# The q, k and v tiles of a hybrid block in pairs by seven block products, the head rows' work among the state-space tiles

## The chip, the cores and the metric

One core of a Trainium2 chip runs the whole block. The metric is the device time of one execution in microseconds (us). Five engines work side by side, each with its own queue, in the order of its program: TensorE (PE, matrix products into PSUM), VectorE (DVE), ScalarE (ACT), GpSimd (POOL) and SyncE (SP, which issues DMAs). They wait for each other by semaphores. SBUF is the working memory of 128 partitions; PSUM has 8 banks of 128 x 512 floats.

## The reference

The block normalises x (1024 tokens x 1024 channels), projects it by one wide matrix `w_in`, and splits the result. The stretch of interest is the projection and the causal convolution behind it, for the state-space branch (`xbc`) and for the DeltaNet branch (`qkv`):

```python
h = rms_norm(x, g_mix_pre[i])
proj = h @ w_in[i]
z, xbc, dt_raw, qkv, gate, b_raw, a_raw, m_gate = jnp.split(proj, IN_SPLITS, axis=-1)
xbc = jax.nn.silu(causal_dwconv(xbc, conv_w) + conv_b)      # 4 taps, 1536 channels
qkv = jax.nn.silu(causal_dwconv(qkv, conv_w))               # 4 taps, 3072 channels
dt = jax.nn.softplus(dt_raw + dt_bias)                      # and g, beta of DeltaNet from a_raw, b_raw
```

Then come the two chunked recurrences, their gated merge, a gated convolutional feed-forward part and a per-layer input embedding. All is float32.

## The kernel before

**Precision and tiles.** Every operand of a product is split into a high and a low part (`w_hi`, `w_lo` of the weights, `act_hi`, `act_lo` of h, all in SBUF), and a product is three matmuls: high x high, high weight x low activation, low weight x high activation. A tile is 128 output channels x 1024 tokens: 8 blocks of 128 input channels x 2 halves of 512 tokens x 3 = 48 matmuls of 512 columns, into one of four buffers of two PSUM banks (`pe_unit`, `pe_steps`, lines 465 to 489).

**Per tile.** SP loads 1 MB of weights for two tiles (`load_block`). POOL makes the high part (line 460) and then the low one (line 462). PE multiplies. DVE copies the tile from PSUM into `xin`, which has three zero columns in front (line 2895), so that the buffer is free at once; the first tap is a `tensor_scalar` on it (line 2902), the other three are `scalar_tensor_tensor` (line 2908) over `xin` and `ring_a`. ACT applies SiLU (line 2813) and stores the tile to the `spill` tensor in DRAM, two in rotation (`spilled`).

**Order.** `PROJ` gives it: 12 state-space tiles, then q and k (16 tiles), v in two runs of 4; all but the first four tiles run in hardware loops of four (`run_tiles`). The head rows (one small tile with dt, a and b in its rows) go through a softplus on DVE (`head_softplus`, 16 dependent operations in `hrow`) behind tile 11; PE turns them to token rows behind q and k (`O_TM`), DVE keeps them (`tm_sources`); PE sums them over the tokens of a chunk behind the first run of v (`O_CUM`), DVE keeps that (`tm_sums`), ACT takes four exponentials. The numbers `O_...` say which use of the four buffers a tile is, `U_...` which use of the weight slots, `Q_...` of the load slots.

**Behind it** (`pe_a`, `dve_a`, `act_a`, `sp_a`, `pool_a`): the z, gate and merge-gate tiles on PE, with the preparation of DeltaNet between their steps. It reads q, k, v of one chunk of tokens back from `spill`, which SP does once all 36 tiles are stored; the first steps of PE that need it stand 15 steps (1.9 tiles) into this stage (`A_START`).

**A stage of the same kind as the change.** The feed-forward stage (`pe_tail`, lines 1820 to 1870) already multiplies its gate and up tiles in pairs by seven products: a matrix of 2 x 2 blocks (output channels x input channels) times one of 2 x 2 blocks (input channels x halves of the tokens) with seven block products instead of eight. Four of the seven weights are sums of weight blocks (`sm`, by DVE, line 2372), ACT makes the high part of each (line 2085), POOL the low one (line 1735). Four of the seven activations are sums of blocks of h, made once (`t1` to `t4`, lines 2349, 2055, 2354). DVE adds the seven products, each one PSUM bank, into the two tiles by seven additions (line 2390), with one product first copied by ACT (`sx`, line 2092). There, ACT takes the first of three taps (line 2068), DVE two (line 2403), on every second pair; on the others DVE multiplies (line 2414).

## Time and profile before

| | |
|---|---|
| median of 3 runs | 2575.64 us (2573.89 to 2580.5) |
| the profiled execution | 2580.09 us, span 2578.4 us |
| PE busy | 2473.8 us, 96% |
| DVE busy | 1541.1 us, 60% |
| POOL busy | 1205.1 us, 47% |
| ACT busy | 720.9 us, 28% |
| DMA | 339.42 MB, mean 132 GB/s |
| PE clock granted | 0.986 of full speed over the span |

The profiled execution is one of its own, and its span leaves out what lies around the program. Busy shares are means over stages with different limits; a wait counts only where it ends last. In the timeline, a matmul's duration overlaps that of the next, so the distance between starts tells its cost. Three stretches matter here: the state-space tiles (69.7 to 200.3 us), q, k, v (200.3 to 461), and the stage behind.

### The profile page before, as it was taken

How to read it: one execution, taken by the hardware profiler on the slowest of the kernel's cores; microseconds unless marked ns; L12 is line 12 of the kernel's file. 1: busy time of each engine (PE TensorE's matmuls, PEld its weight loads, DVE VectorE, ACT ScalarE, POOL GpSimd, SP SyncE). 2: the span in 40 equal slices, each digit the busy share in tenths (PEclk: the TensorE clock that was granted, in tenths of full speed). 3: DMA queues.
4: the chain of work that ended last, by engine and by line, in shares of the span. 5: the costliest groups of instructions: out<-in, count | busy, mean ns of one | idle time of the engine just before them, and what ended most of it. 6: DMA issues, size and time to landing. Idle time of an engine off the chain costs nothing. (4 is left out here: it accounts for less than half of the span.)

```text
span 2578.4 us, 30060 instructions
## 1 busy us (share of the span) xinstructions
PE 2473.8 (96%) x11684; PEld 2044.7 (79%) x11684; DVE 1541.1 (60%) x1361; ACT 720.9 (28%) x828; POOL 1205.1 (47%) x643
## 2 busy tenths in 40 slices
PE   6999999999999999989999789999999999999998
PEld 5888888777778888878877578888888878888786
DVE  4679776435774657654243797776776752322585
ACT  4100101355512233232012443333333330000332
POOL 1433333456544546343346375655565543333563
PEclk8999999999999999999999899999999999999999
DMA  6222222588774666645242312222222253122332
GB/s 201 98 98 90 106 93 103 172 264 273 252 241 139 210 179 194 178 144 180 98 148 97 114 61 87 81 81 81 92 79 73 98 196 115 49 82 82 115 114 106
DMA packets 296703, 339.42 MB, mean 132 GB/s; under 512 B 44493, under 2 KB 253722, under 8 KB 292506
## 3 DMA queue, kind: packets, MB, share of 16 engines
q1 hardware_dynamic: 263754, 275.62, 33.2%
q10 hardware_dynamic: 32848, 62.40, 6.5%
q8 instruction: 71, 1.16, 0.2%
q14 instruction: 30, 0.25, 0.0%
HBM read 234.70 MB, written 103.28 MB: 131 GB/s over the span
## 5 line engine op out<-in xcount | busy, mean ns | idle before, releaser
L475 PE MATMUL ps<-act_hi,w_hi 128*128 128x512 f32 x1712 | 682.9, 399 | 12.8 <-ACT ring_b L955 4.0
L479 PE MATMUL ps<-act_hi,w_lo 128*128 128x512 f32 x1712 | 668.5, 390 | 0.0
L478 PE MATMUL ps<-act_lo,w_hi 128*128 128x512 f32 x1712 | 667.9, 390 | 0.0
L460 POOL TENSOR_SCALAR w_hi<-w_raw 128x1024 fp32r<-128x1024 f32 x161 | 186.2, 1157 | 936.7 <-issue 642.0
L462 POOL TENSOR_TENSOR w_lo<-w_raw,w_hi 128x1024 fp32r<-128x1024 f32 x161 | 437.1, 2715 | 13.4
L475 PEld LDWEIGHTS ps<-act_hi,w_hi 128*128 128x128 f32 x1712 | 322.9, 189 | 85.5 <-issue 11.0
L478 PEld LDWEIGHTS ps<-act_lo,w_hi 128*128 128x128 f32 x1712 | 322.7, 189 | 67.6 <-issue 3.6
L479 PEld LDWEIGHTS ps<-act_hi,w_lo 128*128 128x128 f32 x1712 | 322.2, 188 | 68.2
L1735 POOL TENSOR_TENSOR w_lo<-sm,w_hi 128x512 fp32r<-128x512 f32 x120 | 209.3, 1746 | 100.2 <-ACT w_hi L2085 100.2
L1735 POOL TENSOR_TENSOR w_lo<-w_raw,w_hi 128x512 fp32r<-128x512 f32 x90 | 136.5, 1518 | 131.7 <-ACT w_hi L2085 131.6
L2908 DVE SCALAR_TENSOR_TENSOR ring_a<-xin,par,ring_a 128x1024 f32<-128x1024 f32 x108 | 185.0, 1713 | 11.8 <-DVE ring_a L2902 0.3
L1846 PE MATMUL ps<-t,w_hi 128*128 128x512 f32 x480 | 186.7, 389 | 0.0
L1849 PE MATMUL ps<-t,w_hi 128*128 128x512 f32 x480 | 186.7, 389 | 0.0
L1850 PE MATMUL ps<-t,w_lo 128*128 128x512 f32 x480 | 186.7, 389 | 0.0
L1846 PE MATMUL ps<-act_hi,w_hi 128*128 128x512 f32 x360 | 141.4, 393 | 5.2 <-POOL w_lo L1735 4.8
L1760 PE MATMUL ps<-act_hi,w_hi 128*128 128x512 f32 x320 | 128.6, 402 | 13.6 <-DVE act_lo L2312 6.8
L1849 PE MATMUL ps<-act_lo,w_hi 128*128 128x512 f32 x360 | 140.8, 391 | 0.0
L1850 PE MATMUL ps<-act_hi,w_lo 128*128 128x512 f32 x360 | 140.8, 391 | 0.0
L2813 ACT ACTIVATE ring_b<-ring_a 128x1024 f32<-128x1024 f32 x36 | 38.2, 1062 | 330.9 <-DVE ring_a L2908 330.9
L1763 PE MATMUL ps<-act_lo,w_hi 128*128 128x512 f32 x320 | 125.5, 392 | 0.0
L1764 PE MATMUL ps<-act_hi,w_lo 128*128 128x512 f32 x320 | 125.5, 392 | 0.0
L2474 DVE TENSOR_TENSOR tile<-ps,tile 128x1024 f32<-128x1024 f32 x24 | 29.4, 1224 | 160.8 <-PE ps L479 133.8
(334 smaller groups left out, 4013.0 us busy)
## 6 DMA issues: line engine op xcount, KB each, us to landing
w_raw<-in_w_in_dram SPq DMA_DIRECT2D x34, 1024.0 KB, 5.3
spill<-ring_b ACTq DMA_DIRECT2D x67, 512.0 KB, 2.7
w_raw<-in_w_ffn_down_dram SPq DMA_DIRECT2D x18, 1024.0 KB, 4.8
w_raw<-in_w_ffn_up_dram SPq DMA_DIRECT2D x17, 1024.0 KB, 5.1
w_raw<-in_w_ffn_gate_dram SPq DMA_DIRECT2D x16, 1024.0 KB, 5.1
f_cm<-ring SPq DMA_DIRECT2D x32, 512.0 KB, 2.6
qkv_a<-spill SPq DMA_DIRECT2D x8, 1536.0 KB, 8.3
dec_a<-cum_rows SPq DMA_DIRECT2D x16, 512.0 KB, 14.3
```

The source lines that it names most:

```text
L460: nc.gpsimd.tensor_scalar(hi, raw, 1.0, 0.0, ALU.mult, ALU.add).then_inc(split_done, 1)
L462: nc.gpsimd.tensor_tensor(lo, raw, hi.bitcast(f32), ALU.subtract).then_inc(split_done, 1)
L475: first = nc.tensor.matmul(o, wh, mov[0][:, k, c], start=(k == 0), stop=False)
L478: nc.tensor.matmul(o, wh, mov[1][:, k, c], start=False, stop=False)
L479: last = nc.tensor.matmul(o, wl, mov[0][:, k, c], start=False, stop=(k == KD - 1))
L1735: nc.gpsimd.tensor_tensor(product_slot(w_lo, j), product_in(q, i), product_slot(w_hi, j).bitcast(f32), ALU.subtract).then_inc(w_low[0], 1)
L1760: first = nc.tensor.matmul(dst, wh, mov[0][:, k, in_half(half)], start=(k == 0), stop=False)
L1763: nc.tensor.matmul(dst, wh, mov[1][:, k, in_half(half)], start=False, stop=False)
L1846: first = nc.tensor.matmul(dst, wh[:, k, :], mh[:, k, :], start=(k == 0), stop=False)
L1849: nc.tensor.matmul(dst, wh[:, k, :], ml[:, k, :], start=False, stop=False)
L1850: last = nc.tensor.matmul(dst, wl[:, k, :], mh[:, k, :], start=False, stop=(k == 3))
L2908: v.scalar_tensor_tensor(out=ring_a[:, slot, :], in0=xin[:, slot, tap:tap + SEQ], scalar=col_of(wname, tap * nt + t0 + n), in1=ring_a[:, s ...
```

## The change

Five things, all in the projection:

1. q, k and v are 12 pairs of tiles, each by seven products (`pe_pairs`, `C_PAIRS`), as in the feed-forward stage. DVE makes four weight sums per pair (`dve_sums`), ACT seven high parts (`c_high_of`), POOL seven low parts (`pool_pairs`); DVE evicts by seven additions (`evicts`). A finished tile lies in `xin` or `ring_b` (`c_tile`).
2. The four activation sums `ct1` to `ct4` are made on the way, between the state-space tiles: nine additions and four low parts of 128 x 2048 on DVE, four high parts on ACT.
3. The first tap moves to ACT, for all 36 tiles (`act_first_tap`); DVE has three. The state-space tiles are no longer copied out of PSUM: all taps read PSUM, and the buffer is free behind the third.
4. The head rows' softplus stands behind the first state-space tile, their turn behind the fourth, their sums behind the sixth, and the exponentials with it.
5. The hardware loops are gone: all is written out.

```diff
-    O_QKV = O_XBC + XBC_T
-    O_TM = O_QKV + 16
-    O_QKV1 = O_TM + 2
-    O_CUM = O_QKV1 + 4
-    O_QKV2 = O_CUM + 3
-    O_A = O_QKV2 + 4
+    O_TM, O_CUM = O_XBC + 4, O_XBC + 8
+    O_A = O_XBC + XBC_T + 5
...
+    C_EVICT = {0: (1, 0), 1: (3, 0), 2: (2, 0), 3: (4, 0), 4: (5, 1), 5: (2, 1), 6: (6, 1)}
...
+    def pool_pairs(pool):
+        for p in range(C_PAIRS):
+            for i in range(PRODUCTS):
+                j = PRODUCTS * p + i
+                past(pool, c_high, j + 1)
+                nc.gpsimd.tensor_tensor(c_slot(w_lo, j), c_product_in(p, i), c_slot(w_hi, j).bitcast(f32),
+                                        ALU.subtract).then_inc(c_low[0], 1)
...
+    def pe_pairs(pe):
...
+                elif p % 2:
+                    if i == 0 and p > 1:
+                        past(pe, c_copied, p - 1)
+                    if i == 1:
+                        past(pe, c_copied, p)
+                    if i in (2, 3):
+                        past(pe, c_evicted, SUMMED * (p - 1) + (1, 6)[i - 2])
+                elif i in (0, 1, 5):
+                    past(pe, c_evicted, SUMMED * (p - 1) + {0: 1, 1: 6, 5: 7}[i])
+                wh, wl = c_slot(w_hi, j), c_slot(w_lo, j)
+                mh, ml = moving[i]
+                for k in range(4):
+                    first = nc.tensor.matmul(dst, wh[:, k, :], mh[:, k, :], start=(k == 0), stop=False)
...
+                    nc.tensor.matmul(dst, wh[:, k, :], ml[:, k, :], start=False, stop=False)
+                    last = nc.tensor.matmul(dst, wl[:, k, :], mh[:, k, :], start=False, stop=(k == 3))
+                last.then_inc(c_prod[0], 1)
...
+    def c_high_of(act, p, i):
+
+        j = PRODUCTS * p + i
+        if j < 4:
+            act.wait_ge(unit_begun, U_C + j // 2)
+        else:
+            past(act, c_prod, j - 3)
...
+        def first_tap(t):
+            past(act, c_evicted, SUMMED * (t // 2) + (4, 7)[t % 2])
+            act_first_tap(act, J_Q + t, c_tile(t), pcol("conv_gdn_w", 3 * QKV_T + t), None)
...
+        for p in range(C_PAIRS):
+            for i in range(PRODUCTS):
+                if i == 4:
+                    copy(p)
+                if p or i > 1:
+                    c_high_of(act, p, i)
+                if p and i == 0:
+                    first_tap(2 * p - 2)
+                if p > 1 and i == 2:
+                    silu(2 * p - 3)
+                if p and i == 4:
+                    first_tap(2 * p - 1)
+                if p and i == 5:
+                    silu(2 * p - 2)
...
+        def taps(t):
+            past(dve, c_first, XBC_T + t + 1)
+            src, out = c_tile(t), ring_a[:, (J_Q + t) % 2, :]
+            for n, back in enumerate((1, 2, 3)):
...
+                v.scalar_tensor_tensor(out=out[:, back:SEQ], in0=src[:, 0:SEQ - back], scalar=pcol("conv_gdn_w", (3 - back) * QKV_T + t),
+                                       in1=out[:, back:SEQ], op0=ALU.mult, op1=ALU.add).then_inc(conv_step, 1)
+
+        for p in range(C_PAIRS):
+            evicts(p, (0,))
+            if p:
+                taps(2 * p - 2)
+            evicts(p, (1, 2))
+            if p < C_PAIRS - 1:
+                dve_sums(dve, p + 1)
+            evicts(p, (3, 4, 5))
+            if p:
+                taps(2 * p - 1)
+            evicts(p, (6,))
...
     def pool_a(pool):
         g = nc.gpsimd
-        for m in range(2):
-            split_unit(pool, U_A, m)
+        past(pool, c_prod, PRODUCTS * C_PAIRS - 2)
+        pool.sem_inc(split_done, 2 * QKV_T)
+        split_unit(pool, U_A, 0)
+        past(pool, c_prod, PRODUCTS * C_PAIRS)
+        split_unit(pool, U_A, 1)
...
+        for n in range(XBC_T):
+            b = wait_tile(act, xbc_use(n))
+            if n < 2:
+                act.wait_ge(lo_done, KD)
+            if n == XBC_T - 1:
+                c_high_of(act, 0, 0)
+                c_high_of(act, 0, 1)
+            act_first_tap(act, n, buf(b), pcol("conv_ssm_w", 3 * XBC_T + n), pcol("conv_ssm_b", n))
...
+            act.wait_ge(tile_free[b], uses(xbc_use(n), 0)[1] + 1)
+            act_conv_out(act, n)
...
+        conv(0)
+        head_softplus(dve)
+        for n in (1, 2, 3):
+            conv(n)
+        tm_sources(dve)
+        raw_op(ct1_raw, part(act_hi, 0, 1), part(act_lo, 0, 1), ALU.add)
...
+        dve_sums(dve, 0)
+        dve_pairs(dve)
```

## Rows read from the trace of the kernel before

**Rows 1.** The page, part 1: engine, busy us, share, instructions.

```profile
PE 2473.8 (96%) x11684; PEld 2044.7 (79%) x11684; DVE 1541.1 (60%) x1361; ACT 720.9 (28%) x828; POOL 1205.1 (47%) x643
```

**Rows 2.** By window: busy us (count) of PE, PEld, DVE, ACT, POOL; PEclk, DMA, GB/s.

```profile
69.70:200.30 130.60, 130.60 (x578) 108.15 (x577) 97.89 (x62) 14.02 (x13) 43.16 (x24) 1.00 0.29 101
200.30:460.10 259.80, 259.80 (x1161) 213.96 (x1160) 203.34 (x137) 30.89 (x29) 93.99 (x46) 1.00 0.26 93
460.10:785.00 324.90, 308.42 (x1376) 245.54 (x1375) 172.34 (x211) 142.54 (x130) 167.31 (x81) 0.98 0.76 240
...
1650.00:1950.00 300.00, 300.00 (x1325) 248.50 (x1324) 209.92 (x221) 110.45 (x156) 177.12 (x111) 1.00 0.24 84
```

**Rows 3.** Waits of PE between 60 and 490 us: all there are.

```profile
PE ps L1165 <- ACT hrow L1227: 2.3, 1, 2.3
```

**Rows 4.** Timeline of PE: a tile's first matmul, the next tile's; the chunk sums.

```profile
69.66 0.39 PE L475 MATMUL ps<-act_hi,w_hi 128*128 128x512 f32 x1
...
80.54 0.39 PE L475 MATMUL ps<-act_hi,w_hi 128*128 128x512 f32 x1
...
408.73 1.02 PE L2715 MATMUL ps<-hrow,tri 128*128 128x512 f32 x2
...
417.05 0.79 PE L475 MATMUL ps<-act_hi,w_hi 128*128 128x512 f32 x1
```

**Rows 5.** Timeline of ACT: one tile's SiLU and the issue of its store.

```profile
306.78 1.06 ACT L2813 ACTIVATE ring_b<-ring_a 128x1024 f32<-128x1024 f32 x1 [9.80 <-DVE ring_a L2908]
308.00 0.34 ACTq L2816 DMA_DIRECT2D spill<-ring_b  x1
```

**Rows 6.** Groups by line and shape, feed-forward stage, 1650 to 1950: busy, mean ns.

```profile
L2372 DVE TENSOR_TENSOR sm<-w_raw 128x512 f32<-128x512 f32 x32 | 29.4, 960 | 11.3 <-POOL w_lo L1735 11.3
...
L2372 DVE TENSOR_TENSOR sm<-sm,w_raw 128x512 f32<-128x512 f32 x16 | 24.1, 1504 | 0.0
L2403 DVE SCALAR_TENSOR_TENSOR fa<-xin,par,fa 128x1024 f32<-128x1024 f32 x14 | 23.5, 1680 | 1.0 <-DVE fa L2403 0.5
L2390 DVE TENSOR_TENSOR ring<-ps,sx 128x512 f32<-128x512 f32 x32 | 22.1, 692 | 12.0 <-PE ps L1850 11.3
...
L2085 ACT ACTIVATE w_hi<-w_raw 128x512 fp32r<-128x512 f32 x48 | 30.2, 630 | 59.1 <-PE ps L1850 59.1
...
L2068 ACT ACTIVATE fa<-xin,par 128x1024 f32<-128x1024 f32 x8 | 10.0, 1245 | 25.3 <-DVE xin L2390 25.3
```

**Rows 7.** Timeline of DVE, then of POOL, in the feed-forward stage.

```profile
1722.45 1.27 DVE L2403 SCALAR_TENSOR_TENSOR fa<-xin,par,fa 128x1024 f32<-128x1024 f32 x1
1723.87 2.08 DVE L2403 SCALAR_TENSOR_TENSOR fa<-xin,par,fa 128x1024 f32<-128x1024 f32 x1 [0.15 <-DVE fa L2403]
...
1727.97 3.50 DVE L2403 SCALAR_TENSOR_TENSOR fa<-xinb,par,fa 128x1024 f32<-128x1024 f32 x2
...
1725.89 1.29 POOL L1735 TENSOR_TENSOR w_lo<-sm,w_hi 128x512 fp32r<-128x512 f32 x1 [1.02 <-ACT w_hi L2085]
1728.07 2.33 POOL L1735 TENSOR_TENSOR w_lo<-sm,w_hi 128x512 fp32r<-128x512 f32 x1 [0.89 <-ACT w_hi L2085]
```

**Rows 8.** Groups by line: 490 to 620, 69.7 to 460.1, 1470 to 1600.

```profile
L1295 DVE SCALAR_TENSOR_TENSOR dec_a<-ps,dec_a 128x512 f32<-128x512 f32 x10 | 6.9, 687 | 17.3 <-PE ps L1185 17.3
...
L462 POOL TENSOR_TENSOR w_lo<-w_raw,w_hi 128x1024 fp32r<-128x1024 f32 x35 | 97.8, 2795 | 2.9
...
L2354 DVE TENSOR_TENSOR t<-t_raw,t 128x2048 fp32r<-128x2048 f32 x4 | 10.5, 2670 | 0.0
```

**Rows 9.** Busy time of DVE alone over the softplus chain.

```profile
198.00:223.00 25.00, 24.52 (x16) 1.00 0.19 65
```

**Rows 10.** Timelines of DVE and ACT where q, k, v end.

```profile
461.21 1.23 DVE L2895 COPY xin<-ps 128x1024 f32<-128x1024 f32 x1 [2.89 <-PE ps L479]
...
469.30 1.06 ACT L2813 ACTIVATE ring_b<-ring_a 128x1024 f32<-128x1024 f32 x1 [9.82 <-DVE ring_a L2908]
...
482.57 2.00 ACT L1227 ACTIVATE hrow<-qkv_a 128x1024 f32<-128x1024 f32 x2 [9.39 <-DMA qkv_a<-spill]
```

More of the change, by code:

```diff
@@ L384, in uses_spilled @@
         return 16 * len(range(slot, j_end, 2))
-    def run_tiles(eng, tiles, j0, body):
-        if j0 == 0:
-            for n in range(tiles):
-                body(None, n)
-        else:
-            with eng.Fori(0, tiles // 4) as it:
-                for n in range(4):
-                    body(it, n)
     def uses(o0, n, it=None, per=0):
@@ L2687, in _, with head_rows_to_tokens, head_sums @@
         mov = (act_hi, act_lo)
-        def unit(it, n, j0, o0):
-            if j0 or n:
-                pe_unit(pe, 1 + j0, o0, n, it, 4, mov=mov)
-            if j0 == 0 and n == 1:
+        def head_rows_to_tokens():
+            for i, (row, step) in enumerate(((1, HEAD_SP), (2, HEAD_L))):
+                pe.wait_ge(head_dve, step)
+                b = wait_buffer(pe, O_TM, i)
+                for c in range(NCH):
+                    last = nc.tensor.transpose(buf(b)[:, c * P:(c + 1) * P], hrow[:, row, c * P:(c + 1) * P], ident[:, :])
+                last.then_inc(tile_done[b], 1)
+        def head_sums():
+            pe.wait_ge(tm_dve, TM_SRC)
+            lg, lb = hrow[:, 0, :], hrow[:, 3, :]
+            b = wait_buffer(pe, O_CUM, 0)
+            for half in range(2):
+                c = slice(half * 512, half * 512 + 512)
+                nc.tensor.matmul(ps[:, 2 * b + half, :], tri[:, :], lg[:, c], start=True, stop=False)
+                last = nc.tensor.matmul(ps[:, 2 * b + half, :], ident[:, :], lb[:, c], start=False, stop=True)
+            last.then_inc(tile_done[b], 1)
+            b = wait_buffer(pe, O_CUM, 1)
+            for ch in range(NCH):
+                c = slice(ch * P, ch * P + P)
+                nc.tensor.matmul(buf(b)[:, c], lg[:, c], tri[:, :], start=True, stop=False)
+                last = nc.tensor.matmul(buf(b)[:, c], lb[:, c], ident[:, :], start=False, stop=True)
+            last.then_inc(tile_done[b], 1)
+            b = wait_buffer(pe, O_CUM, 2)
+            for half in range(2):
+                c = slice(half * 512, half * 512 + 512)
+                last = nc.tensor.matmul(ps[:, 2 * b + half, :], ones[:, :], lg[:, c], start=True, stop=True)
+            last.then_inc(tile_done[b], 1)
+        for n in range(XBC_T):
+            if n:
+                pe_unit(pe, 1, xbc_use(n) - n, n, mov=mov)
+            if n == 1:
                 for o in (O_SMALL, O_XBC0, O_P[1]):
@@ L2828, in _ @@
+        act_pairs(act)
         act_a(act)
@@ new lines, in conv @@
+        def conv(n):
+            past(dve, c_first, n + 1)
+            o = xbc_use(n)
+            b, c = uses(o, 0)
+            src, out = buf(b), ring_a[:, n % 2, :]
+            for i, back in enumerate((1, 2, 3)):
+                if i:
+                    dve.wait_ge(conv_step, 2 * n + i)
+                v.scalar_tensor_tensor(out=out[:, back:SEQ], in0=src[:, 0:SEQ - back], scalar=pcol("conv_ssm_w", (3 - back) * XBC_T + n),
+                                       in1=out[:, back:SEQ], op0=ALU.mult, op1=ALU.add
+                                       ).then_inc(conv_step if i < 2 else tile_free[b], 1)
+            if n == 0:
+                dve.wait_ge(tile_free[b], c + 1)
+                v.sem_inc(tile_free[b], UNUSED[b])
@@ new lines, in part, with raw_op, sum_low @@
+        def part(src, k, half):
+            return src[:, 4 * k:4 * k + 4, half * 512:half * 512 + 512].bitcast(f32)
+        raw_step = [0]
+        def raw_op(out, x, y, op):
+            past(dve, c_traw, raw_step[0])
+            v.tensor_tensor(out[:, :, :], x, y, op).then_inc(c_traw[0], 1)
+            raw_step[0] += 1
+        def sum_low(t, raw, highs):
+            past(dve, c_thigh, highs)
+            v.tensor_tensor(t[:, 1], raw[:, :, :], t[:, 0].bitcast(f32), ALU.subtract).then_inc(c_tlow[0], 1)
@@ new lines, in _ @@
+        conv(5)
+        tm_sums(dve)
+        past(dve, c_traw, 5)
+        sum_low(ct1, ct1_raw, 1)
+        conv(6)
+        dve.wait_ge(tm_act, 4)
+        for at, i, row, n in TM_COLS:
+            v.tensor_copy(tmc[:, :, at:at + n], tmh[:, :, i, row:row + n]).then_inc(tm_kept, 1)
+        dve.wait_ge(tm_kept, len(TM_COLS))
+        dve.wait_ge(cum_kept, 16)
+        raw_op(ct3_raw, ct2_raw[:, :, :], part(act_hi, 0, 0), ALU.subtract)
+        raw_op(ct3_raw, ct3_raw[:, :, :], part(act_lo, 0, 0), ALU.subtract)
@@ L2918, in _ @@
+        conv(7)
+        raw_op(ct4_raw, part(act_hi, 1, 0), ct2_raw[:, :, :], ALU.subtract)
+        raw_op(ct4_raw, ct4_raw[:, :, :], part(act_lo, 1, 0), ALU.add)
+        conv(8)
+        past(dve, c_traw, 9)
+        sum_low(ct3, ct3_raw, 3)
+        sum_low(ct2, ct2_raw, 3)
+        conv(9)
+        sum_low(ct4, ct4_raw, 4)
+        conv(10)
+        conv(11)
+        dve_sums(dve, 0)
+        dve_pairs(dve)
         dve_a(dve)
```

314 lines of the change are left out of this document (199 added, 115 removed).

## Prediction

> **What bounds the kernel now.** I read the busy shares first: TensorE (PE) is busy 96% of 2578.4 us [rows 1]. Then the stages. The change touches 69.7 to 460.1: there PE is busy 130.60 of 130.60 us and 259.80 of 259.80 us, VectorE (DVE) 98 and 203 [rows 2]. Over that stretch PE's only wait comes at its far end, 2.3 us for ScalarE's (ACT) squares [rows 3]. So every microsecond of PE work taken away is one gained, as long as nobody else is late. One tile of 128 channels takes PE from 69.66 to 80.54, 10.88 us for 48 products, 0.2267 us each [rows 4]; the rows' 0.39 overlap each other.
>
> The second question is how much room the others have. DVE waits for PE ahead of a tile (2.89 us ahead of the last [rows 10]) and ACT ahead of each SiLU (9.80 [rows 5]). The kernel's feed-forward stage already runs such seven-product pairs, and there PE is busy 300.00 of 300.00 us with DVE at 210 and POOL at 177 [rows 2]. That stage is my yardstick for prices, but it has two taps per tile, on half its pairs (with a multiply per tile), where the changed stage has three taps on every tile.
>
> **What is removed.** The 24 q, k, v tiles cost PE 24 x 10.88 = 261.1 us. As 12 pairs of 7 products of 12 matmuls they cost 12 x 84 x 0.2267 = 228.5 (19.04 a pair). Gain if PE never waits: 32.6 us. DVE loses per tile the copy out of PSUM (1.23 [rows 10]) and the first tap; ACT takes the tap, 1.25 us [rows 6].
>
> **The pair stage: DVE per pair.** Seven evictions from PSUM at 0.69 are 4.8 us; four weight sums of 512 columns; six taps of 1024 columns. What do the last two cost? The rows of one stretch tell [rows 7]. A tap with POOL quiet takes 1.27; the next, with POOL at work, 2.08. POOL's subtraction alone takes 1.29, and 2.33 when it starts 0.10 after a DVE tap (1727.97, 1728.07): it ends 1.16 after that tap would have. So a two-operand SBUF operation of DVE and POOL's operation take turns, whole. Evictions, with one operand in PSUM, are 0.69 whatever POOL does [rows 6]. The means under this are 0.96 for a sum of two weight blocks, 1.50 for one that also reads a sum just made, 1.68 for a tap [rows 6].
>
> The Trainium skill ("SBUF — State Buffer", Who interferes with whom) says the same and speaks against this change: a DVE instruction with two SBUF inputs contends with a GpSimd instruction that reads SBUF, and the one that comes second fully blocks. The trace agrees (2.33 against 1.29 above). Were the access shared without turns, the sum would be rival A's.
>
> Claims on the shared access per pair: POOL 7 x 1.29 = 9.0, taps 6 x 1.27 = 7.6, sums 4 x 0.69 (an eviction's length, estimate) = 2.8: 19.4 us, already over PE's 19.04. For the feed-forward stage, two pairs: POOL 18.1, eight sums 5.5, four taps 5.1, two multiplies priced as taps 2.5: 31.2 of 38.1, 18% of it free.
>
> On top there is a ping-pong. In `act_pairs` the SiLU of the odd tile stands ahead of `copy(p)`, and DVE's first eviction of pair p waits for `copy(p)`. So after DVE's last tap of tile 2p-3: SiLU 1.06, DMA issue 0.34 and its gaps 0.1 [rows 5], a weight copy 0.63 [rows 6], the PSUM copy about the same: 2.7 us, of which DVE fills 0.7 with its seventh eviction and idles 2.0. DVE's ring per pair is then
>
> - low end, the prices of the feed-forward stage: 4.8 + 3 x 0.96 + 1.50 + 6 x 1.68 + 2.0 = 21.3;
> - high end: in a full ring all seven POOL operations meet a DVE one, each delaying it by up to 1.1 (2.33 - 1.29 = 1.04 the other way round): 4.8 + 2.8 + 7.6 + 7 x 1.1 + gaps 0.3 = 23.2, with part of the 2.0 inside it.
>
> I laid the three queues side by side by these prices and got 22 to 23; I take 22.4, since the ring leaves POOL nothing but DVE's busy time to work in. DVE's lateness reaches PE through banks (product 1 or 3 waits for the sixth eviction) and through ACT, where a first tap stands ahead of the next weight copy. The first pair has no taps, the second few: 21.4 (with the wait below) and 19.0. Stage: 21.4 + 19.0 + 10 x 22.4 = 264.4 against 261.1: **+3.3**. The whole gain is spent.
>
> **The state-space tiles (12 tiles, 130.6 us).** Taps now read PSUM; nearest row: the same operation from PSUM, 512 columns, 0.69 [rows 8], so 1.24 for 1024, three are 3.8. Bounds: 1.2 and 1.7 (as in SBUF with POOL); I take 1.24, as the operand is in PSUM. A buffer is now held until the third tap. Four things cost PE:
>
> 1. The softplus chain, 24.5 us of DVE [rows 9], moves from behind tile 11, where PE had four buffers, to behind tile 0. With the end of tile 0 as zero, conv 0 ends at 5.3; the chain, beside two POOL splits (2.8 each [rows 8]) that hold it up by 1.8 each, at 33.4; conv 1 at 37.2. PE, done with tile 3 at 32.6 and with one turn of the head rows at 33.6, waits for tile 1's buffer: **3.6**.
> 2. ACT and DVE now alternate: SiLU 1.06, issue 0.4, next first tap 1.25, three taps 3.8. Conv 2 ends at 43.7; PE's tile 4 needs its buffer from 38.2 on: **5.6**.
> 3. Tile 6 needs tile 5's buffer, behind nine ACT/DVE steps and the operand differences: conv 5 ends at 75.3; PE ends tile 5 at 65.5 and its sums, 8.3 us in this trace (408.73 to 417.05 [rows 4]), at 73.8: **1.5**. The 13 passes over 2048 columns, at 2.67 each (34.7 us of DVE) [rows 8], otherwise fit in DVE's idle time.
> 4. The first two weight copies of the pairs are issued by ACT only after tile 11 is complete: copy 0.63, POOL 1.29, latencies 0.3: **2.2**; then product 2 waits for SiLU 11 behind conv 11: 2.4, counted in the first pair above.
>
> Sum **+12.9**. The head rows' matmuls and exponentials only move; ACT has the time for them. The two weight streams (SP) have the landing time they had; unrolled loops cost nothing PE would see, as its queue is full.
>
> **Behind the stage.** PE starts unit z 0 without a wait (eviction 6 of pair 11 is early, its weights' split, 1.1 and 2.8, has two products' 5.4 us). But two tiles' taps are left after PE's last product: eviction, six taps, SiLU end 12.6 us later, against 9.4 before (461.0, from DVE's start at 461.21, to 470.4 [rows 10]). The loading of q, k, v hangs on it, and ACT's squares, for which PE waits already [rows 3]: **+3.2**.
>
> **Sum.** -32.6 + (264.4 - 228.5 = 35.9) + 12.9 + 3.2 = +19.4 us. The profiled execution took 2580.09 (span 2578.4), the median is 2575.64; on the median: **2595**. At 21.3 a pair it is 2584, at 23.2, 2603; a PE clock that falls in the longer waits (0.98 granted in the stage behind, with such waits [rows 2]) adds up to 5.
>
> **Rivals.**
> A. *Faster: the access is not the bound.* DVE and POOL fall into step so that POOL works beside evictions and in DVE's pauses, as the multiplies of the feed-forward stage do; PE sets 19.04 a pair. Decides if blocking costs DVE under 1.5 us a pair. 2575.6 - 32.6 + 2.4 + 12.9 + 3.2 = 2562. For: that stage's 100%. Against: 19.4 over 19.04 and the ping-pong. 0.13.
> B. *Half and half:* 20.4 a pair, 10 x 2.0 less, 2575; no difference. 0.13.
> C. *Dearer:* every POOL operation blocks and the ring adds the 2.0, 24.5 a pair: 2616; or taps out of PSUM cost 1.7 and the clock falls. 0.09.
> D. *The gain isn't there at all* because products cost more than 12 x 0.2267; the feed-forward rows exclude it: under 0.01, in C.
> Forecast (21.3 to 23.2 a pair, 2584 to 2603): 0.65.
>
> **Chances.** 0.3% is 7.7 us, about what this measurement can tell from no change. Faster (under 2568): A, 0.13. Same: B and a small part of the forecast, 0.15. Slower: 0.72. The range leaves out A and the far half of C: 2568 to 2608.
>
> **What would show it.** Per pair: the stretch between first products of successive pairs, 22.4 (A: 19.0); DVE busy over 90% in the pair stage; taps at 1.8 to 2.1 mean; PE waits for `ps` evictions or `w_lo`, one or two a pair. In the first stage: two PE waits of some 4 and 6 us near 105 to 115 us, ended by DVE. Wrong if taps' mean is below 1.6, if DVE has pauses other than behind `copy`, or if PE's waits in the tiles lie elsewhere.

## The result and the profile after

The changed kernel takes 2603.11 us in the median of six runs (2595.09 to 2610.0), beside 2577.36 for the kernel before in the same set (2569.52 to 2581.01). The ratio is 1.0099, with a 95% interval of 1.0078 to 1.012: slower by 20 to 31 us. The forecast was 2595, 19.4 over before; sign and range held, and the middle was 8 us low.

All rows of the kernel after come from one execution of 2598.74 us (span 2597.0), which lies 4.4 under its median. The page, part 1 (columns as in [rows 1]):

```profile
PE 2452.3 (94%) x11540; PEld 2013.7 (78%) x11540; DVE 1564.0 (60%) x1434; ACT 822.8 (32%) x964; POOL 1261.1 (49%) x679
```

PE has 21.5 us less work than in [rows 1], and yet the span is 18.6 longer. Busy times by window, columns as in [rows 2], from 69.70 to the first product of the pairs, then the pairs:

```profile
69.70:210.70 141.00, 131.02 (x580) 106.35 (x578) 109.26 (x80) 40.23 (x35) 39.79 (x21) 0.96 0.24 85
210.70:475.90 265.20, 237.73 (x1008) 186.77 (x1008) 226.79 (x199) 101.47 (x140) 149.96 (x85) 1.00 0.25 89
```

Where PE was busy for all of it in [rows 2], it now idles 10 us in the first window and 27.5 in the second. Who ends this idle time is told by the waits of PE between 60 and 520 us (total, times, longest), the answer to [rows 3]:

```profile
PE ps L590 <- POOL w_lo L558: 29.5, 31, 2.1
PE ps L1398 <- ACT hrow L1462: 5.5, 1, 5.5
PE ps L489 <- DVE ring_a L3133: 5.0, 1, 5.0
PE ps L2920 <- DVE ring_a L3133: 2.9, 1, 2.9
PE ps L489 <- POOL w_lo L476: 1.7, 1, 1.7
```

31 short waits for low parts, nearly three a pair, are the pairs' loss. POOL ends these waits but is not short of time: it has 115 us of idle time in the stage itself. Its own waits there are for ACT's high parts, ACT's for DVE's taps, and DVE's waits for ACT between 200 and 490 us are these (its others, 14.9 us in all, are for PE's products):

```profile
DVE ring_a L3133 <- ACT ring_a L605: 12.8, 2, 8.0
DVE ring_b L696 <- ACT csx L642: 10.9, 5, 2.2
DVE xin L696 <- ACT csx L642: 9.4, 5, 2.2
```

The first belongs to the last state-space tiles. The second and third are one wait per pair, 2.2 us for ACT's copy of sum x. The timelines of DVE, then ACT, where one pair follows another show what it is made of:

```profile
367.69 2.20 DVE L704 SCALAR_TENSOR_TENSOR ring_a<-ring_b,par,ring_a 128x1021 f32<-128x1021 f32 x1
369.81 0.68 DVE L696 TENSOR_TENSOR xin<-ps,csx 128x512 f32<-128x512 f32 x1
372.66 0.69 DVE L696 TENSOR_TENSOR ring_b<-ps,csx 128x512 f32<-128x512 f32 x1 [2.17 <-ACT csx L642]
...
369.92 1.06 ACT L610 ACTIVATE ring_a<-ring_a 128x1024 f32<-128x1024 f32 x1 [4.76 <-DVE ring_a L704]
371.01 0.33 ACTq L612 DMA_DIRECT2D spill<-ring_a  x1
371.44 0.63 ACT L626 ACTIVATE w_hi<-csm 128x512 fp32r<-128x512 f32 x1 [0.46 <-ACT ring_a L610]
371.98 0.58 ACT L642 ACTIVATE csx<-ps 128x512 f32<-128x512 f32 x1
```

DVE's last tap lets the SiLU go (369.92); behind the SiLU stand a DMA issue, a high part and the copy; at 372.66 DVE goes on. Then the prices of DVE's operations, groups by line and shape between 250 and 450 us (count, busy, mean ns), the answer to [rows 6]:

```profile
L704 DVE SCALAR_TENSOR_TENSOR ring_a<-ring_b,par,ring_a 128x1022 f32<-128x1022 f32 x9 | 19.7, 2188 | 0.3
L677 DVE TENSOR_TENSOR csm<-csm,w_raw 128x512 f32<-128x512 f32 x9 | 15.9, 1764 | 0.0
...
L696 DVE TENSOR_TENSOR xin<-ps,csx 128x512 f32<-128x512 f32 x18 | 12.4, 689 | 11.2 <-ACT csx L642 8.7 <-PE ps L594 2.2
```

Two of a tile's three taps take 2.19 us (here that of 1022 columns; the one of 1021 is the same, and the first, of 1023, is at 1.28), a sum that reads the sum before it takes 1.76, evictions out of PSUM 0.69 as before.

One number serves for all comparisons below: the time from the first product of state-space tile 1, where the touched stages begin, to the point where PE begins the sums of squares of the first chunk, where they end. Before, it runs from 69.66 ([rows 4]) to 483.88, 414.2 us. After, it begins at

```profile
67.45 0.39 PE L489 MATMUL ps<-act_hi,w_hi 128*128 128x512 f32 x1
```

and ends at 503.95, 436.5 us. The begin has to be taken from each trace: it lies between 67.45 and 70.42 in kernels whose programs are the same up to there. The ratio column is against the kernel before on the same chip, in the same set.

| kernel | tile 1 begins | squares' sums begin | the time between, against before | median us | ratio (95%) |
|---|---|---|---|---|---|
| before | 69.66 | 483.88 | | 2577 to 2582 in all sets | |
| after | 67.45 | 503.95 | +22.3 | 2603.11 | 1.0099 (1.0078 to 1.012) |
| copy first | 70.40 | 480.38 | -4.2 | 2575.93 | 0.9981 (0.9967 to 0.9995) |
| short low parts | 70.42 | 476.76 | -7.9 | 2575.32 | 0.9975 (0.9961 to 0.9989) |
| interleaved | 67.96 | 468.96 | -13.2 | 2566.17 | 0.9945 (0.9925 to 0.9966) |
| softplus in pieces | 67.92 | 496.14 | +14.0 | 2597.37 | 1.0066 (1.0048 to 1.0083) |
| plain tiles | 69.46 | 492.08 | +8.4 | 2586.48 | 1.0017 (0.9999 to 1.0034) |
| plain, pieces | 67.91 | 484.09 | +2.0 | 2580.29 | 0.9995 (0.9985 to 1.0006) |
| all orders | 69.81 | 463.81 | -20.2 | 2562.07 | 0.9924 (0.9906 to 0.9941) |
| all orders, tail | 67.70 | 457.22 | -24.7 | 2555.87 | 0.9901 (0.9882 to 0.992) |
| the same, squares later | 69.58 | 461.27 | -22.5 | 2585.86 | 1.002 (1.0008 to 1.0032) |
| interleaved, all, tail | 67.92 | 452.94 | -29.2 | 2548.52 | 0.9877 (0.9849 to 0.9905) |

In all but one row the ratio, times 2577, agrees with the trace's difference within 4 us: what is won or lost by the squares stays won or lost. The exception is its own lesson.

### The profile page after: what moved, and what is told of

Its sections match the earlier page's. It is cut to its first block and busy times, and to the rows that moved or that the text cites. A ratio compares the mean times of both kernels' runs of the same rounds, so it can differ in the third digit from the quotient of the medians.

```text
span 2597.0 us, 29659 instructions
## 1 busy us (share of the span) xinstructions
PE 2452.3 (94%) x11540; PEld 2013.7 (78%) x11540; DVE 1564.0 (60%) x1434; ACT 822.8 (32%) x964; POOL 1261.1 (49%) x679
## 5 line engine op out<-in xcount | busy, mean ns | idle before, releaser
L489 PE MATMUL ps<-act_hi,w_hi 128*128 128x512 f32 x1328 | 534.0, 402 | 19.0 <-DVE ring_a L3133 5.0
L474 POOL TENSOR_SCALAR w_hi<-w_raw 128x1024 fp32r<-128x1024 f32 x137 | 167.2, 1220 | 763.5 <-issue 647.4
L493 PE MATMUL ps<-act_hi,w_lo 128*128 128x512 f32 x1328 | 520.2, 392 | 0.0
L492 PE MATMUL ps<-act_lo,w_hi 128*128 128x512 f32 x1328 | 519.4, 391 | 0.0
L476 POOL TENSOR_TENSOR w_lo<-w_raw,w_hi 128x1024 fp32r<-128x1024 f32 x137 | 366.6, 2676 | 11.4
L489 PEld LDWEIGHTS ps<-act_hi,w_hi 128*128 128x128 f32 x1328 | 250.9, 189 | 77.5 <-issue 12.4
L493 PEld LDWEIGHTS ps<-act_hi,w_lo 128*128 128x128 f32 x1328 | 250.5, 189 | 53.3
L492 PEld LDWEIGHTS ps<-act_lo,w_hi 128*128 128x128 f32 x1328 | 250.8, 189 | 52.9 <-issue 3.6
L2075 PE MATMUL ps<-act_hi,w_hi 128*128 128x512 f32 x360 | 141.9, 394 | 6.4 <-POOL w_lo L1964 4.5
L1989 PE MATMUL ps<-act_hi,w_hi 128*128 128x512 f32 x320 | 130.0, 406 | 14.6 <-DVE act_lo L2541 6.8
L2078 PE MATMUL ps<-act_lo,w_hi 128*128 128x512 f32 x360 | 141.5, 393 | 0.0
L2079 PE MATMUL ps<-act_hi,w_lo 128*128 128x512 f32 x360 | 141.5, 393 | 0.0
L1992 PE MATMUL ps<-act_lo,w_hi 128*128 128x512 f32 x320 | 126.1, 394 | 0.0
L1993 PE MATMUL ps<-act_hi,w_lo 128*128 128x512 f32 x320 | 126.0, 394 | 0.0
L2314 ACT ACTIVATE w_hi<-sm 128x512 fp32r<-128x512 f32 x120 | 75.4, 630 | 141.9 <-PE ps L2079 138.5
L2363 ACT ACTIVATE act_hi<-f_raw 128x1024 fp32r<-128x1024 f32 x32 | 31.2, 1047 | 255.1 <-DMA f_raw<-f_cm 255.1
```

The lines of the kernel that those rows point to most:

```text
L474: nc.gpsimd.tensor_scalar(hi, raw, 1.0, 0.0, ALU.mult, ALU.add).then_inc(split_done, 1)
L476: nc.gpsimd.tensor_tensor(lo, raw, hi.bitcast(f32), ALU.subtract).then_inc(split_done, 1)
L489: first = nc.tensor.matmul(o, wh, mov[0][:, k, c], start=(k == 0), stop=False)
L492: nc.tensor.matmul(o, wh, mov[1][:, k, c], start=False, stop=False)
L493: last = nc.tensor.matmul(o, wl, mov[0][:, k, c], start=False, stop=(k == KD - 1))
L1989: first = nc.tensor.matmul(dst, wh, mov[0][:, k, in_half(half)], start=(k == 0), stop=False)
```

## Experiment 1: the copy ahead of the SiLU

My theory T was the ring of the prediction: DVE's taps, ACT's SiLU, ACT's copy, DVE's evictions, with DVE and POOL taking turns on top. The rivals: DVE's work as such is the bound, or order matters nowhere.

```diff
                 if i == 4:
                     copy(p)
+                if i == 4 and p > 1:
+                    silu(2 * p - 3)
                 if p or i > 1:
                     c_high_of(act, p, i)
...
-                if p > 1 and i == 2:
-                    silu(2 * p - 3)
```

> One thing is changed against the changed kernel: in a steady pair ScalarE makes the copy of sum x (behind high part 3) before the SiLU of tile 2p-3 and not after it. Theory T (ring of turns): in the kernel after, VectorE waits some 2.2 us a pair for this copy (two waits of 2.2 us in its rows between 200 and 490 us have five each), and that wait is part of the ring that sets 22.6 us a pair; the copy comes some 1 us earlier, the blocks of VectorE and GpSimd fall otherwise in step, and a pair takes 19.0 to 21.0 us, the whole 12 to 35 us less than after. Rival R1 (VectorE's own work is the bound): VectorE is 86% busy in the stage, the order of ScalarE's queue moves nothing but idle time, a pair stays at 22.2 to 22.6 us, the whole within 5 us of after. Rival R2 (the copy is not what is late): the time is as after and another engine ends the same wait.

Measured: 2575.93 us, 0.9981 against the kernel before where the changed kernel has 1.0099. One statement in one queue takes back the whole loss, and a hair more. The copies of successive pairs start 19.5 us apart (315.48, 334.96, 354.43, 373.90) where they were 22.6 apart (326.78, 349.38, 371.98). Busy times of the engines between 300 and 390 us in this kernel:

```profile
300.00:390.00 90.00, 89.45 (x391) 72.75 (x390) 88.88 (x80) 40.76 (x56) 55.75 (x33) 1.00 0.31 111
```

DVE is now busy 88.9 of 90 us: it is the bound, at 19.5 us a pair, and not at 22.2 or more as R1 had it. The 3.1 us a pair are the 2.2 of waiting and 0.9 of blocking: one of the two runs of three taps takes 4.8 us where it took 5.7, as one POOL operation less falls on it. On PE's side, two of its waits until 530 us:

```profile
PE ps L1398 <- ACT hrow L1462: 10.4, 1, 10.4
...
PE ps L590 <- POOL w_lo L558: 3.3, 6, 2.1
```

The waits for low parts fell from 29.5 to 3.3 us, but 4.9 us of that came back at the squares (10.4 where it was 5.5): PE reaches them earlier, and what they wait for, the last tiles' taps, SiLU and way through memory, did not shorten as much.

## Experiment 2: POOL's low parts shortened

```diff
-nc.gpsimd.tensor_tensor(c_slot(w_lo, j), c_product_in(p, i), c_slot(w_hi, j).bitcast(f32),
+nc.gpsimd.tensor_tensor(c_slot(w_lo, j)[:, :, 0:8], c_product_in(p, i)[:, :, 0:8],
+                        c_slot(w_hi, j)[:, :, 0:8].bitcast(f32),
```

> The low parts of the weights of the seven products of each pair are made for 8 of every 128 columns only, so that GpSimd's operation there falls from 1.7 to 2.0 us to a few tenths; the rest of those low parts is left out (the products then use old numbers), all other work stands. Theory T (VectorE's two-operand operations and GpSimd's stand behind each other in turns): VectorE's sums fall from 1.67 to 1.76 us to 1.3 us, its blocked taps from 2.19 to 1.3 us, and VectorE's work of a pair goes under TensorE's own pace of 19.04 us: 19.0 to 19.6 us a pair, 36 to 43 us less than after. Rival R1 (VectorE's operations are long of themselves, from their operands' place): taps stay at 2.19 us and the pair at 22 us or more; the whole is within 5 us of after.

Measured: 2575.32 us, 0.9975. A pair takes 19.04 us (copies at 317.31, 336.35, 355.39), to the hundredth PE's own 84 products of 0.2267, with no wait of PE at all from 230 to 440 us. Groups of DVE and POOL in that stretch (DVE 250 to 450, POOL 250 to 440):

```profile
L704 DVE SCALAR_TENSOR_TENSOR ring_a<-ring_b,par,ring_a 128x1022 f32<-128x1022 f32 x10 | 12.8, 1283 | 0.4
...
L558 POOL TENSOR_TENSOR w_lo<-csm,w_hi 128x32 fp32r<-128x32 f32 x40 | 23.0, 574 | 82.4 <-ACT w_hi L626 82.4
```

The same tap on the same operands takes 1.28 us where it took 2.19 (the others 1.28 to 1.47), and the sum that took 1.76 takes 0.74, because POOL's operation beside them takes 0.57 in place of some 1.7 to 2.0. That settles that the taps are long for POOL's sake, as the page "SBUF — State Buffer" of the Trainium skill has it (Who interferes with whom). ACT's order was untouched here, so the ping-pong alone is no bound either: the ring needs both. The whole time missed what was expected (28 us under the changed kernel by the medians, 32 by the ratios, not 36 to 43), since the squares wait 10.4 us here too.

## Experiment 3: the same work, interleaved on VectorE

Is it the place of the copy, or how the blocks fall? Here ACT's order is that of the changed kernel and only DVE's is different.

```diff
-            evicts(p, (0,)); taps(2p-2); evicts(p, (1, 2)); dve_sums(p+1)
-            evicts(p, (3, 4, 5)); taps(2p-1); evicts(p, (6,))
+            # a, b: taps of tiles 2p-2, 2p-1; e: evictions; s: sums of pair p+1
+            a1 e0 a2 s1 a3 s3 e1 e2 s2 s4 e3 b1 b2 e4 b3 e5 e6
```

(The diff is in short form; each letter is one of the instructions that stood there before.)

> ScalarE's order is again that of the changed kernel (the copy of sum x after the SiLU). Only VectorE's order in a pair is changed: the three taps of a tile and the four sums are no longer run one behind the other but with evictions between them (tap, eviction 0, tap, sum s1, tap, sum s3, evictions 1 and 2, sums s2 and s4, eviction 3, tap, tap, eviction 4, tap, evictions 5 and 6); the work is the same. Theory T (VectorE's two-operand operations and GpSimd's low parts stand behind each other in turns, so what a pair costs hangs on how they fall against each other): first product of a low part and the copy come at their time, 19.0 to 19.6 us a pair in place of 22.6; the squares' wait is 7 to 10 us; 2568 to 2577 us in all, 29 to 38 under the changed kernel's some 2606. Rival R1 (the work, not its order, makes 22.6): a pair stays over 22 us. Rival R10 (only the place of the copy in ScalarE's queue counts, since VectorE waits for it at its first eviction): 22.0 to 22.6 us a pair here, as that place is unchanged.

Measured: 2566.17 us, 0.9945. A pair takes 19.04 us (copies at 331.53, 350.58, 369.63, 388.67) with the copy where it always was. DVE's timeline over part of a pair:

```profile
362.27 3.03 DVE L710 SCALAR_TENSOR_TENSOR ring_a<-xin,par,ring_a 128x1023 f32<-128x1023 f32 x2
365.22 0.69 DVE L699 TENSOR_TENSOR csx<-ps,csx 128x512 f32<-128x512 f32 x1
365.82 1.72 DVE L710 SCALAR_TENSOR_TENSOR ring_a<-xin,par,ring_a 128x1021 f32<-128x1021 f32 x1
367.46 1.28 DVE L699 TENSOR_TENSOR ring_b<-ps,csx 128x512 f32<-128x512 f32 x2
368.66 1.27 DVE L710 SCALAR_TENSOR_TENSOR ring_a<-ring_b,par,ring_a 128x1023 f32<-128x1023 f32 x1
371.47 0.69 DVE L699 TENSOR_TENSOR xin<-ps,csx 128x512 f32<-128x512 f32 x1 [1.54 <-PE ps L594]
372.08 1.35 DVE L710 SCALAR_TENSOR_TENSOR ring_a<-ring_b,par,ring_a 128x1022 f32<-128x1022 f32 x1
```

Between most taps there is now an eviction, which reads PSUM; POOL can work beside it. By the groups of 250 to 450 us, a pair's six taps take 9.0 us where they took 11.3. The last tap of tile 2p-3 is also earlier, so the SiLU and the copy are done before DVE comes to eviction 0; it now waits 1.54 us for PE itself. R1 and R10 are out: neither the amount of work nor the place of the copy by itself makes 22.6. It takes both together, the run of blocked taps right ahead of the SiLU and the copy behind that SiLU: experiment 1 changed the one, this run the other, and each was enough. This order does two things at once, less blocking and an earlier last tap, and their shares are not told apart. This is also the prediction's rival A in the flesh: in this order DVE and POOL do fall in step. The squares' wait was 2.0 us where I expected 7 to 10; the first A tile waits 2.5 us for an eviction instead, which I had not worked out. The whole came out under the 2568 to 2577 that I expected.

## Experiment 4: the softplus in pieces

```diff
         conv(0)
-        head_softplus(dve)
-        for n in (1, 2, 3):
+        steps = head_softplus(dve)        # a "yield" behind each of its steps
+        for n, count in ((1, 2), (2, 6), (3, 8)):
+            for _ in range(count):
+                next(steps, None)
             conv(n)
```

> The softplus of the head rows on VectorE is cut: two of its steps stand before the taps of state-space tile 1, six before tile 2, the rest before tile 3, in place of all before tile 1. Theory T: the waits of TensorE of 2.9 and 5.2 us between 100 and 111 us and the stretch from 104.4 to 114.6 us with a granted clock of 0.5 come from VectorE, which is late with the taps behind its softplus of 27 us; both go, and the first product of the pairs starts 8 to 13 us earlier; the whole is 8 to 13 us less than after. Rival R3 (the lateness is only moved: VectorE has no slack in these tiles, and what it does not do before tile 1 it owes before tile 4): the waits return further on, the first product starts within 2 us of where it did. Rival R4 (the low clock belongs to the head rows' small matmuls and not to the waits): the 10 us at 0.5 stay, and only 3 to 8 us are gained.

Measured: 2597.37 us, 1.0066, some 8 us under the changed kernel by the ratios. The first product of the pairs starts at 203.16 and not at 210.69, which is 135.2 us behind that of tile 1 where it was 143.2. PE's timeline at the second turn of the head rows, of the kernel after and then of this one:

```profile
104.00 1.58 PE L2920 MATMUL ps<-ident,hrow 128*128 128x128 f32 x8 [2.87 <-DVE ring_a L3133]
110.63 0.80 PE L489 MATMUL ps<-act_hi,w_hi 128*128 128x512 f32 x1 [5.04 <-DVE ring_a L3133]
111.22 0.63 PE L492 MATMUL ps<-act_lo,w_hi 128*128 128x512 f32 x1
111.65 0.63 PE L493 MATMUL ps<-act_hi,w_lo 128*128 128x512 f32 x1
```

```profile
103.28 1.96 PE L2930 MATMUL ps<-ident,hrow 128*128 128x128 f32 x16 [2.56 <-DVE hrow L776]
...
105.32 0.39 PE L492 MATMUL ps<-act_lo,w_hi 128*128 128x512 f32 x1
105.55 0.39 PE L493 MATMUL ps<-act_hi,w_lo 128*128 128x512 f32 x1
```

Of 2.9 and 5.0 us of waiting, one wait of 2.6 is left, for the head rows themselves, and nothing comes back further on: R3 is out. In the rows of after the matmuls behind the waits follow each other at 0.43 us, against 0.23 in this kernel, which has the same small matmuls of the head rows: the 10 us at the lower clock are gone, and R4 is out. One wait alone can bring the lower clock too, as the last section shows. From tile 1 to the squares the gain was 8.3 us in the trace, at the lower end of the 8 to 13 I gave.

## Experiment 5: plain tiles, with the other half of the change

```diff
-        pe_pairs(pe)
+        for t in range(QKV_T):
+            pe_unit(pe, U_C, O_C, t, mov=mov)
...
-        dve_pairs(dve)
+        for t in range(QKV_T):
+            conv(XBC_T + t)        # three taps out of PSUM
```

The feeding code on the other engines goes back in the same way, and the sums of x and the operand differences of the pairs are left out with them. The second kernel adds the edit of experiment 4.

> The pairs are undone: the 24 q, k and v tiles go as plain tiles of eight products in two column blocks each, as in the kernel before. What else the change made is kept: the head rows' work stands in the state-space tiles and VectorE reads all taps out of PSUM. Theory T (by the sums of the prediction: the pairs themselves give and take about nothing, +35.9 us of ring against 32.6 us saved in matmuls, and the loss is that of the state-space tiles and the tail): 2585 to 2597 us in the median, 7 to 20 us over before and 5 to 18 us under after; the stage of the plain tiles runs with no wait of TensorE at its own pace. Rival R5 (the state-space part costs nothing on its own, its waits are made good behind it): within 5 us of before. Rival R6 (the pairs are worth having, and the other part costs it all): over 2600 us.

> As the run with plain tiles (2586.5 us), and the softplus in pieces of 2, 6 and 8 steps before the taps of tiles 1, 2 and 3. Theory T: the waits of 2.9 and 5.3 us of TensorE and the stretch at the lower clock make up all of that run's loss against before; with the pieces at most one wait of 2.6 us is left, and taps read out of PSUM leave no wait at the first squares: 2574 to 2580 us, within 0.3% of before or a little faster. Rival R9 (that run's +4.4 us are something else, as the taps' reads of PSUM): within 2 us of the run with plain tiles.

Measured: 2586.48 us (1.0017) for the plain tiles, 2580.29 (0.9995) with the softplus in pieces. Waits of PE between 60 and 500 us in the first, then in the second:

```profile
PE ps L490 <- DVE ring_a L3125: 5.3, 1, 5.3
PE ps L2915 <- DVE ring_a L3125: 2.9, 1, 2.9
```

```profile
PE ps L2925 <- DVE hrow L777: 2.6, 1, 2.6
```

The plain tiles keep 1.0017 of 1.0099, or 4.4 us over before (0 to 9 by the interval), where theory T gave 7 to 20 and R5 less than 5; the trace has +8.4. So the ratio does not tell T from R5. The trace does: the two waits (8.2 us) and the lower clock behind them (granted 0.50 from 108 to 116 us) are there in full, and what makes some of it good is not in the change at all. These plain q, k and v tiles have their taps read out of PSUM and no copy ahead of them, and so the last SiLU ends 6.2 us after PE's last product and not 9.4 as in [rows 10]: ACT's first tap starts at 471.87, as soon as the product is there, and the SiLU ends at 478.03.

```profile
471.87 1.12 ACT L604 ACTIVATE ring_a<-ps,par 128x1024 f32<-128x1024 f32 x1 [4.72 <-PE ps L494]
476.97 1.06 ACT L611 ACTIVATE ring_a<-ring_a 128x1024 f32<-128x1024 f32 x1 [3.98 <-DVE ring_a L3125]
```

PE finds its squares ready, and the 2.3 us of [rows 3] are gone. Without that gain the state-space half would stand at 10.7 us in the trace, and the pairs' half has the other 11.6 of 22.3: 265.2 for 261.1 in the stage, 2.1 for the first low part of the pairs, 1.7 for that of the A tiles, 3.2 more at the squares, which make 11.1. Both halves cost, and by the trace about the same.

With the pieces the waits up to 500 us are down to 2.6, and the sum is nil: within 0.1% of before, 5.7 us under the plain tiles by the ratios, so R9 is out. I had hoped for up to 6 us less; the interval allows 4 at most.

## Experiment 6: all orders, the tail, and one step too far

```diff
-        head_softplus(dve)                 # all 15 steps before tile 1
+        2, 5, 4, 5 steps before tiles 1, 2, 3, 4
-            if n == 3: head_rows_to_tokens()
-            if n == 5: head_sums()
+            if n == 4: head_rows_to_tokens()
+            if n == 6: head_sums()
...
+            if n == XBC_T - 1: c_high_of(act, 0, 0) ... c_high_of(act, 0, 3)   # ahead of the SiLU of tile 11
```

With the copy first as in experiment 1, and the tail of the second kernel:

```diff
             evicts(p, (1, 2))
             if p < C_PAIRS - 1:
                 dve_sums(dve, p + 1)
+            else:
+                taps(2 * p - 1)
             evicts(p, (3, 4, 5))
...
+            if p == C_PAIRS - 1:
+                taps(2 * p)
             evicts(p, (6,))
-        taps(QKV_T - 2)
         taps(QKV_T - 1)
```

> All of the change, with the orders that theory T asks for: the copy of sum x ahead of the SiLU (as in the run with the copy first, 2575.9 us), the softplus of the head rows in pieces of 2, 5, 4 and 5 steps before the taps of tiles 1 to 4, the head rows' turns behind tiles 4 and 6 in place of 3 and 5, and the first four high parts and the first sums of the pairs made a little earlier. Theory T: no wait of TensorE over 1 us before the first product and no fall of its clock; the squares of the first A tile still wait 10.4 us for ScalarE, since the tail is as it was. From 2575.9: 9 less as in the run with the softplus in pieces (2597.4 against some 2606), 4 less for the two waits of 2.2 and 2.3 us about the first product: 2560 to 2566 us. Rival R3 (lateness moved on): waits of 3 to 5 us come back behind tile 4 or 6, 2568 to 2575 us.

> As the run with all orders, and the tail: in the last pair the taps of tile 21 stand where the sums of the next pair stood, and those of tile 22 before the last eviction, so that only those of tile 23 are left behind the last product. Theory T: the squares' wait of 10.4 us for ScalarE (SiLU of the last tile, spill, load) falls by the three taps and a SiLU that no longer stand behind the last product, to 5 to 8 us: 2556 to 2562 us. Rival R7 (the wait is that of the load's way out and back, 9.4 us of idle time on ScalarE, and not of the taps): it stays at 9 to 10.5 us and the time within 2 us of the run with all orders.

Measured: 2562.07 us (0.9924) and 2555.87 (0.9901), the first inside what was expected, the second just under it. In the first, PE has no wait at all before the pairs, so R3 is out here too. PE's waits between 60 and 470 us in the kernel with the tail (the third and last is 0.3 us):

```profile
PE ps L1411 <- ACT hrow L1475: 4.5, 1, 4.5
PE ps L489 <- POOL w_lo L476: 1.7, 1, 1.7
```

The squares' wait was 10.5 us without the tail. R7 is out: the load's way out and back (9.30 us of ACT's idle time ahead of the squares) stays, but it starts earlier.

The third kernel puts products in front of the wait:

```diff
-    A_START = [15, 27, 40, 55, 70, 85, 100, 116]
+    A_START = [20, 32, 45, 58, 71, 85, 100, 116]
```

> As the run with the tail, and the sums of squares of the first chunk come after step 20 of the A tiles' products in place of step 15 (a step is six matmuls, 1.36 us, so 6.8 us of products are put in front of the wait); the turns of chunks 1 to 4 go back by 3, 5, 5 and 1 steps (32, 45, 58, 71), to keep the hand-written order in step. Theory T: what is left of the squares' wait goes, nothing else moves: 5 to 7 us less than the run with the tail, 2550 to 2557 us. Rival R8 (the wait is moved: what hangs on the squares is late by 6.8 us for the next stage, or the first chunks crowd each other): waits of 3 to 7 us appear elsewhere in the A tiles, and the time is within 2 us of the run with the tail or over it.

Measured: 2585.86 us, 1.002: 30 us lost against the kernel with the tail, far beyond R8's size. PE's waits between 60 and 530 us (a third group is 0.6 us in all):

```profile
PE ps L489 <- ACT ring_b L1466: 11.7, 2, 11.2
PE ps L489 <- POOL w_lo L476: 11.5, 2, 9.8
```

The squares find their data ready, as I wanted. The first loss is the 9.8 us for low parts, before the product at 500.80: POOL stood 15.6 us for the load of the weights. It does so in the kernel with the tail as well (13.6 us, to the same load), where PE is held 1.4 us by it; why the later turns lay it open I have not followed. The second is seen in ACT's queue, which runs squares, roots, decays and the out-copies of the A tiles in one fixed order. `squares(2)` waits 16.46 us for the load of q, k and v of its chunk, which SP issues at 515.02 where it did so at 500.49 in the kernel with the tail; behind it stands the out-copy of an A tile, and that copy frees a PSUM buffer, for which PE stands 11.2 us at 526.90:

```profile
526.90 0.79 PE L489 MATMUL ps<-act_hi,w_hi 128*128 128x512 f32 x1 [11.18 <-ACT ring_b L1466]
...
522.51 2.00 ACT L1475 ACTIVATE hrow<-qkv_a 128x1024 f32<-128x1024 f32 x2 [16.46 <-DMA qkv_a<-spill]
...
525.82 1.02 ACT L1466 ACTIVATE ring_b<-ps 128x1024 f32<-128x1024 f32 x1
```

A wait of 4.5 us was traded for 21, and behind each of the two the clock is granted at 0.50 (500 to 504 and 524 to 528 us). I moved five chunks' turns at once, so which of them does the harm isn't told apart.

## Experiment 7: the version that beats both

Experiment 3's order on DVE, the orders of experiment 6 and its tail, and ACT's copy after the SiLU.

> As the run with all orders and the tail (2555.9 us), but with VectorE's interleaved order in the pairs and ScalarE's copy after the SiLU. Theory T: 19.1 to 19.3 us a pair in place of 19.5, 3 to 4 us over nine steady pairs; the tail as in that run, the squares' wait 3 to 6 us: 2550 to 2555 us. Rival R11 (the tail depends on the order of the last pairs, and the waits for the first low parts of the A tiles grow by what the pairs gain): 2555 to 2558 us.

Measured: 2548.52 us, 0.9877 (0.9849 to 0.9905): 1.2% under the kernel before, 2.2% under the kernel as changed, a little under the 2550 to 2555 that I expected, and R11 is out. A pair takes 19.05 us (copies at 316.15, 335.19, 354.24, 373.28). By the ratio 31.7 us are won, by the trace up to the squares 29.2, so the products' saving of 32.6 is there nearly whole. What is left to win up to the squares is the wait of 4.4 us for them and 1.1 for the first A tile's weights:

```profile
PE ps L1413 <- ACT hrow L1477: 4.4, 1, 4.4
```

## Why the prediction was right, step by step

**Pairs, 22.4 us and 264.4 in all: right, for the reason given.** Measured 22.6 and 265.2. By its parts: the idle time behind the copy was 2.17 us for 2.0; the second and third taps 2.19, the first 1.28, a mean of 1.89 between the 1.68 of the feed-forward stage and the full blocking of the high end; evictions 0.69. Experiments 1 to 3 show the mechanism: take away POOL's length, the ping-pong, or the run of blocked taps, and 22.6 falls to 19.0 or 19.5. That the stage came out within 1 us is in part luck, as two errors cancel: pairs 0 to 3 took 88.2 us (210.69 to 298.86) and not 85.2, and the last pair about 19 in place of 22.4; it has no sums left to make.

**State-space tiles, +12.9: 13.1 measured.** From tile 1's first product at 67.45 to that of the pairs at 210.69 it is 143.2 us, less eleven tiles of 10.88 and the head rows' 10.5 (what the kernel before spends from 69.66 to 461.01 over its 35 tiles). The waits were 2.9 for 3.6, 5.0 for 5.6, none for the 1.5 before tile 6, and 2.1 for 2.2. Each was forecast a little large, and that of tile 6 was wrong. What made up for it was the clock, which the prediction named only as "up to 5", outside the sum: 2.5 us, from 8 transposes in 1.58 us (1.03 for the turn before) and 4.00 us for nine matmuls that need 2.04. So the size of this term is right partly by luck. Waits and clock add up to 12.5; the other 0.6 I have not followed. The "12 tiles (130.6 us)" of the prediction's heading is a slip: the window from 69.7 to 200.3 holds eleven state-space tiles and the first of q, and no term uses it.

**Tail, +3.2: right in size, by a different sum, and so by luck.** The squares wait 5.5 us for 2.3. But the last SiLU ends 15.7 us after PE's last product (12.6 forecast): the three taps ahead of the last eviction took 7.00 us and the six behind it 9.28, where 1.27 each is the unblocked price. The 3.1 us more did not reach the squares, since PE itself had lost 1.7 us to a wait for the A tiles' low part, which the prediction had at none ("two products' 5.4 us"), and since the way from the SiLU's end to the squares was 11.1 us where it was 12.2.

**The sum.** From tile 1 to the squares the trace has +22.3 us for +19.4 forecast: 13.1 for 12.9, 4.1 for 3.3, 1.7 for nothing, 3.2 for 3.2. Behind that point the eight sums of squares take 5.26 us for 3.67. The median ratio says 20 to 31, and holds both; that the profiled execution's span is only 18.6 longer comes in part from tile 1, which starts 2.2 us earlier in it.

**The rivals.** A's price was right: with DVE and POOL in step the pairs run at PE's 19.04. It only needed another order. What I had wrong there was its deciding condition. "Claims of 19.4 us on the shared access against 19.04" was an argument against A, yet experiments 3 and 7 run at 19.04 with the same operations. Some of what I counted as claims doesn't collide, so the sum of claims is no floor. Nor did blocking have to fall under 1.5 us a pair: in experiment 3 the taps cost 1.4 over six of 1.27, and one sum of the four stays at 1.66 where 0.69 is unblocked, 2.4 in all.

**The signs.** Two would have misled a reader: DVE was to be busy over 90% and is 86% (226.79 of 265.20, the 2.17 of idle time a pair and a thinner start), and PE's waits come nearly three a pair, not one or two. The taps' mean, the wait behind the copy (DVE's only one in a steady pair), and the two waits in the first stage are where they were said to be.

## What to carry to other kernels

When a change removes work from the bounding engine, lay the queues of the others side by side before judging it: here 32.6 us were saved and 36.7 lost in the same stage, most of it to a ring of two engines. Moving one statement turned 1.0% slower into 0.2% faster; interleaving the same VectorE instructions, so that fewer of those with two SBUF operands stand in a row, into 0.6% faster; with the orders of experiment 6 on top it was 1.2%. A long wait behind a helper engine names the last link only; follow it until an engine waits for one that waits for it. And a wait at the end of a stage was cut here by starting its chain earlier, while pushing the waiting turns back in a fixed order, which the other queues keep, cost far more than the wait.
